# Turning and splitting the residual block by block behind the output projection of a hybrid decoder layer

## The chip, the cores and the metric

One Trainium2 chip, one core of it. The metric is the device time of one execution in microseconds (us). The kernel is one program with one instruction stream per engine: TensorE (PE; PEld is its weight load), VectorE (DVE), ScalarE (ACT), GpSimd (POOL), and SyncE (SP), which here only issues DMA transfers. Engines wait for each other by semaphores; an engine executes its own stream strictly in order, so whatever stands behind a waiting instruction waits too.

## What is computed

One layer of a decoder for 512 prompt tokens and 8 sample tokens together (T = 520 tokens, model width 1024 = 8 blocks of 128 channels). A combined input projection feeds three branches (spatial gating MLP, gated DeltaNet, cross-attention); their gated sum goes through `w_o` and is added to the residual. Then comes a mixture of experts, 4 groups of 8, of which each token takes the top group and two experts in it. The end of the layer, which is what the change is about, is in the reference:

```
x = x + (g_a * o_a + g_b * o_b + g_c * o_c) @ p['w_o']
x = x + hier_moe(rmsnorm(x, p['norm_ffn']), p)
...
grp_logits = (t @ p['w_router_group'] + p['b_router_group']).astype(F32)
g_idx = jnp.argmax(grp_logits, axis=-1)
exp_logits = (t @ p['w_router_expert'] + p['b_router_expert']).astype(F32)
top_v, top_i = lax.top_k(in_grp, TOP_K)
act = jax.nn.silu(gate) * up * combine[:, gi, :, None]
```

All inputs and outputs are fp32. Besides the two residual streams the layer returns memory keys and values, the DeltaNet states (`gdn_s` for the samples), and the last rows of the convolution.

## The kernel before, in words

**Layout.** Activations lie channel-major: the 128 partitions are channels of a block, tokens run along the free axis. SBUF is cut by hand into named regions (`RA`, `M`, `ZG`, `HT`, `CQ`, `MKV`, `RAW`, `X`) that many tensors share one after another; `place` puts a tensor into one.

**Order of work.** A list, `SCHEDULE`, made by `make_schedule` (line 125), gives one order of events. Every engine walks through this list and executes its share of each event, so an engine's order is the order of the list, and the engines meet through semaphores. There is no planner that decides at run time.

**Dense projections.** Weights come in 52 blocks of 1 MiB (`load_block`, line 598) into a ring of three `raw` buffers. ScalarE rounds a block to its high part `w_h` (line 1510), VectorE subtracts to get the low part `w_l` (line 2069), and every product is three: high with high, high with low, low with high (line 900). The last four blocks are `w_o`. Their tiles are numbered `WO_TILE + k`, k = 0 to 7, one for each block of 128 output channels. From k = 2 on a tile comes in two parts of 24 products, so that other work can be put between them. ScalarE's `w_h` and VectorE's `w_l` of the next weight block stand in their streams at part 0 of each even k. When a tile is done VectorE adds the residual: `x1[k]` (line 2143).

**Between the output tiles** stand the updates of the sample states: `sd_diag` (ScalarE, eight copies with a scale, line 1782), `sd_outer` (two products on TensorE, line 1359, then VectorE's addition, line 2462, which also releases the PSUM tensor), `sd_decay` (VectorE, line 2456), and the store of each head by SP (line 627). `f_prep` of block k scales `x1` by `norm_ffn` and rounds it on ScalarE (`hr_h`, line 1792), squares it (line 1793), and has VectorE make the low part `hr_l` (line 2468); GpSimd sums the squares (line 1978). `r_mm` (line 1370) adds the block's share of the 36 router logits, again in three products for each half of the tokens, with the logits on partitions. `f_table` lets GpSimd fill the constants of the expert stage.

**Behind the last tile.** `f_norm` sums the squares per token (line 1380); the logits are copied out and transposed to token rows (lines 1796, 1386); VectorE picks group and experts in a chain of small dependent operations (lines 2481 to 2517) that ends in `hit`; `rank` (line 1430) counts with products of 0 and 1 at which place of its expert's list each token stands; VectorE then has the number of rounds (line 2531), each token's rank, and with `one_hot` the selection matrix `sel` (line 2540). Beside that, `h_in` and `h_sub` turn `x1`, scaled by `norm_ffn`, into five token tiles of 104 rows, which are split into three bf16 parts `h2p` (lines 1406 to 1422 on TensorE, 1808 on ScalarE, 2522 on VectorE).

**Expert stage.** Experts go in 16 pairs. For a pair TensorE gathers the chosen tokens (`gather`, line 1066: 120 products of `h2p` with `sel`; for the first pair `first_gather`, line 1086), ScalarE copies them to `xt` (line 1830), then come gate, up and down products (line 1095), 32 each. A pair needs `e_gate` and `e_up` (4 MiB each) and two `e_down` (2 MiB each), one buffer of each kind. SP reloads a buffer when its last user has finished (`load_pair`, line 633); the loads of the second pair are cut in halves (`load_second`, line 652) and the first of them waits for half of the first pair's gate products (`half_mm`). The first pair itself is loaded by `load_pair(0)`: `e_up` when all output tiles are done, `e_gate` after the logits, `e_down` after `f_norm` and the last `sd_outer`. Results go out by indirect DMA to `y_rows`; the last pair's rows and the residual are added in the final stage, which also normalizes and stores `y`.

## Time and profile before

| | |
|---|---|
| time, median of 3 runs | 1384.88 us (1384.71 to 1386.62) |
| span of the profiled execution | 1385.7 us |
| TensorE busy / weight loads | 1295.6 us (93%) / 1011.1 us (73%) |
| VectorE, ScalarE, GpSimd busy | 485.1, 451.6, 141.1 us |
| chain that ended last, by engine | PE 66%, DMA 20%, DVE 6%, ACT 5%, issue 2% |
| mean granted TensorE clock | 0.983 of full speed |
| HBM read, written | 295.80 MB, 25.10 MB |

The span runs from the first to the last instruction of one profiled execution; the page gives no other time for that execution. TensorE runs at one of two clocks, 1.2 or 2.4 GHz; the granted clock is given as a share of the full one. "Idle before" names what ended the idle time of an engine in front of an instruction; "issue" means that the profile shows nothing it waited for. A busy TensorE is not TensorE at its peak, since products are pipelined and their ends modelled. In the chain, the pieces from about 776 to 841 us are the output projection, those to 872 us the router and the first gather, those to about 1348 us the experts.

### The profile page before, as it was taken

The numbers are of one execution on the slowest core, as the hardware profiler recorded it, in microseconds if no ns is written. First come the engines' busy times: TensorE is split into PE (matmuls) and PEld (weight loads), VectorE is DVE, ScalarE is ACT, GpSimd is POOL, SyncE is SP. The second block draws the span as 40 slices with busy tenths as digits, with TensorE's granted clock in tenths as the row PEclk, the third lists the DMA queues.
The fourth block names the chain that finished last, engine by engine and source line by source line (L and its number), as shares of the span: only waits on it lengthen the run. The fifth ranks groups of instructions, "written<-read, shape, count | busy, mean of one in ns | idle before, by whom it ended". The sixth has DMA issues, their size and how long they took to land.

```text
span 1385.7 us, 24097 instructions
## 1 busy us (share of the span) xinstructions
PE 1295.6 (93%) x10407; PEld 1011.1 (73%) x10407; DVE 485.1 (35%) x882; ACT 451.6 (33%) x775; POOL 141.1 (10%) x208
## 2 busy tenths in 40 slices
PE   3999999899999998989999899999999999999997
PEld 3999988688999998779999888544454444454435
DVE  6332243433346556742344876210010100010003
ACT  5532223443234466344447664101111111011012
POOL 2320000000122211100111112010000000000010
PEclk9999999999999999989999999999999999999999
DMA  5235327533162133432113347899999999999983
GB/s 213 74 108 163 116 94 316 212 140 120 64 222 92 61 100 100 132 100 84 54 39 112 151 154 321 329 401 429 429 431 431 431 431 428 429 431 431 429 284 83
DMA packets 67152, 317.69 MB, mean 229 GB/s; under 512 B 29987, under 2 KB 38563, under 8 KB 44277
## 3 DMA queue, kind: packets, MB, share of 16 engines
q1 hardware_dynamic: 64765, 312.54, 57.8%
q0 software_dynamic: 2304, 3.94, 0.7%
q8 instruction: 65, 1.06, 0.3%
q14 instruction: 18, 0.15, 0.0%
HBM read 295.80 MB, written 25.10 MB: 232 GB/s over the span
## 4 chain that ended last, share of the span: by engine, by line
PE 66%; DMA 20%; DVE 6%; ACT 5%; issue 2%; SPq 0%; POOL 0%; DVEq 0%; ACTq 0%
PE pp L900 34%; DMA e_up<-in_w_up 17%; PE pp L1095 14%; PE pp L1066 2%; PE pp L950 2%; DMA e_down<-in_w_down 1%; DVE w_l L2069 1%; PE pp L1269 1%; PE pp L1289 1%; DMA raw<-in_w_blk 1%; PE pp L1297 1%; ACT w_h L1510 1%; PE pp L1202 1%; PE pp L1454 1%; PE pp L1464 1%
## 5 line engine op out<-in xcount | busy, mean ns | idle before, releaser
L900 PE MATMUL pp<-ht_h,w_h 128*128 128x260 f32 x1280 | 270.6, 293 | 9.1 <-DVE ht_l L2188 9.1
L900 PE MATMUL pp<-ht_h,w_l 128*128 128x260 f32 x1280 | 260.4, 285 | 0.0
L900 PE MATMUL pp<-ht_l,w_h 128*128 128x260 f32 x1280 | 260.4, 285 | 0.0
L900 PEld LDWEIGHTS pp<-ht_h,w_h 128*128 128x128 f32 x1280 | 200.6, 192 | 14.6 <-issue 14.0
L900 PEld LDWEIGHTS pp<-ht_l,w_h 128*128 128x128 f32 x1280 | 200.5, 192 | 0.0
L900 PEld LDWEIGHTS pp<-ht_h,w_l 128*128 128x128 f32 x1280 | 200.1, 191 | 0.0
L2069 DVE TENSOR_TENSOR w_l<-raw,w_h 128x2048 fp32r<-128x2048 f32 x52 | 120.8, 2324 | 103.6 <-ACT w_h L1510 103.5
L1095 PE MATMUL pp<-e_up,xt 128*64 128x512 f32 x512 | 116.6, 609 | 18.1 <-DMA e_up<-in_w_up 18.1
L1095 PE MATMUL pp<-e_down,act_t 128*64 128x512 f32 x512 | 115.1, 602 | 3.3 <-DMA e_down<-in_w_down 3.3
L1510 ACT ACTIVATE w_h<-raw 128x2048 fp32r<-128x2048 f32 x52 | 99.5, 1914 | 56.7 <-PE pp L900 53.1
L1095 PE MATMUL pp<-e_gate,xt 128*64 128x512 f32 x512 | 112.6, 592 | 1.2 <-ACT xt L1830 1.2
L1095 PEld LDWEIGHTS pp<-e_up,xt 128*64 128x64 f32 x512 | 36.3, 140 | 96.1 <-issue 67.7
L1066 PE MATMUL pp<-sel,h2p 104*128 104x128 bf16 x1800 | 105.4, 219 | 0.0
L1066 PEld LDWEIGHTS pp<-sel,h2p 104*128 104x128 bf16 x1800 | 101.9, 98 | 0.2
L1095 PEld LDWEIGHTS pp<-e_gate,xt 128*64 128x64 f32 x512 | 36.8, 137 | 73.8 <-issue 73.5
L1095 PEld LDWEIGHTS pp<-e_down,act_t 128*64 128x64 f32 x512 | 36.3, 138 | 70.2 <-issue 68.7
L2594 DVE SCALAR_TENSOR_TENSOR act_r<-pp,slot_r,sg 128x512 f32<-128x512 f32 x16 | 12.0, 751 | 213.2 <-PE pp L1095 213.2
L2606 DVE TENSOR_SCALAR y_sb<-pp,slot_w 128x512 f32<-128x512 f32 x16 | 12.0, 751 | 202.7 <-PE pp L1095 202.7
L2135 DVE SCALAR_TENSOR_TENSOR cacc<-xpad,params,cacc 128x512 f32<-128x512 f32 x72 | 62.1, 863 | 56.2 <-ACT cacc L1566 54.5
L1842 ACT ACTIVATE act_t<-pp 128x512 f32<-128x512 f32 x16 | 9.6, 597 | 199.7 <-PE pp L1137 199.7
L2013 POOL TENSOR_TENSOR fill<-fill 128x1 f32<-128x1 f32 x47 | 16.3, 353 | 435.8 <-DVE y_sb L2606 273.3
L1563 ACT ACTIVATE xpad<-pp 128x520 f32<-128x520 f32 x24 | 14.5, 605 | 77.5 <-PE pp L900 77.4
(451 smaller groups left out, 1685.8 us busy)
## 6 DMA issues: line engine op xcount, KB each, us to landing
e_up<-in_w_up SPq DMA_DIRECT2D x16, 4096.0 KB, 22.6
e_gate<-in_w_gate SPq DMA_DIRECT2D x15, 4096.0 KB, 20.8
e_down<-in_w_down SPq DMA_DIRECT2D x30, 2048.0 KB, 15.6
raw<-in_w_blk SPq DMA_DIRECT2D x52, 1024.0 KB, 5.1
kv_ring<-in_cache_k SPq DMA_DIRECT2D x8, 1024.0 KB, 5.6
kv_ring<-in_cache_v SPq DMA_DIRECT2D x8, 1024.0 KB, 4.8
s_ring<-in_state_gdn SPq DMA_DIRECT2D x16, 512.0 KB, 5.3
y_rows<-zero_y SPq DMA_DIRECT2D x10, 416.0 KB
```

The lines of the kernel that those rows point to most:

```text
L900: last = mm(dst, w_[:, k, cs], x_[:, k, ts], start=(k == 0 and q == 0), stop=(k == KD - 1 and q == 2))
L950: last = mm(out[:, u, :], lhs(u), rhs(u), start=True, stop=True)
L1066: last = mm(pp[0][:, k // 4, (k % 4) * 128:(k % 4 + 1) * 128], src[:, t, k * 128:(k + 1) * 128], sel[:, t, :, :], start=(i == 0), stop=(i ...
L1095: last = mm(out[rows], lhs[:, rows], w, start=start, stop=stop, skip_group_check=True)
L1202: last = mm(ob[:, c, :], av_tok[:, c, g * 128:(g + 1) * 128], ws_t[:, g, :], start=False, stop=(c == NCH - 1))
L1269: last = mm(dst, qc[:, 2 * h + dc, c * CH:(c + 1) * CH], mk[:, 2 * h + dc, :], start=(dc == 0), stop=(dc == 1))
L1289: last = mm(side[:, dc, :], mv[:, mt, cc:cc + 128], prob_t[:, mt, :], start=(mt == 0), stop=(mt == 1))
L1510: fn(w_h[b % 2][:], raw[b % 3][:], ACT.Copy).then_inc(hi_ready, 1)
L1563: fn(whole(xpad[t % 2][:, 3:3 + T]), ps, ACT.Copy).then_inc(conv_copy, 1)
L2013: return tt(fill[:, 4 + i:5 + i], fill[:, 3:4], fill[:, 3:4], ALU.mult)
L2069: tt(w_l[b % 3][:], raw[b % 3][:], w_h[b % 2][:].bitcast(F32), ALU.subtract).then_inc(lo_ready, 1)
L2135: ins = stt(c_[:, 0:SEQ], x_[:, tap:tap + SEQ], param("w_conv", 4 * SLOT[t] + tap), c_[:, 0:SEQ], ALU.mult, ALU.add)
```

## The change

- **Turned per block.** `x1` is no longer scaled and turned in five token tiles behind the projection. In ten parts (`PARTS`) it is transposed as it is, four 104x128 pieces at a time, into one PSUM bank (`turn_x`); eight of the parts stand between the output tiles, two behind the last. ScalarE rounds the bank to bf16 (first of `h2p`), VectorE subtracts that from the bank (`x_remainder`, `x_rest`), ScalarE rounds the remainder (`x_middle`), and GpSimd subtracts again (`x_lowest`). The next part's transposes wait for the remainder, since there is one bank. `h_in`, `h_sub`, `first_gather`, `gain_d`, `zero_b` and `minus_b` go.
- **Gain elsewhere.** `norm_ffn` is multiplied into the router weights (GpSimd, `w_r_gain`) and into `xt`, which VectorE now writes instead of ScalarE.
- **Logits** are five fp32 products per block with the tokens as stationary side, straight to token rows; `hr_h`, `hr_l`, the split router weights and the transposition of the logits go.
- **`sd_diag`** of odd heads moves to GpSimd, one operation; five of the `sd_outer` steps (heads 3 to 7) move one half tile later.
- **Homes.** `e_gate` lies in `RA`, `e_down[0]` in `ZG`, `h2p` in `HT`, the small tensors of the expert stage in `CQ`. The first pair is loaded in six pieces: `e_down[0]` at `sd_outer` 5, three quarters of `e_up` behind the last state store, and the rest, with `e_gate`, when all output tiles are done. The final loads of `yt` wait for `oh_mm` too.

```diff
+PARTS = [0, 1, 2, 3, "b0", 4, 5, 6, 7, "b1"]
+NPART = len(PARTS)
...
-    out += [("sd_diag", 0), ("w_r_split",), ("f_prep", 0), ("f_prep", 1), ("sd_decay", 0), ("sd_diag", 1)]
-    outers = {(2, 1): 0, (3, 0): 1, (3, 1): 2, (4, 0): 3, (4, 1): 4, (5, 0): 5, (5, 1): 6, (6, 0): 7}
+    out += [("sd_diag", 0), ("w_r_gain",), ("f_prep", 0), ("f_prep", 1), ("sd_decay", 0), ("sd_diag", 1)]
+    outers = {(2, 1): 0, (3, 0): 1, (3, 1): 2, (4, 1): 3, (5, 0): 4, (5, 1): 5, (6, 0): 6, (6, 1): 7}
+    turns = {(2, 0): (0,), (2, 1): (1,), (3, 0): (2,), (4, 0): (3,), (4, 1): ("b0",), (5, 0): (4,), (6, 0): (5,), (7, 0): (6,)}
     for k in range(2, KD):
         for p in range(2):
             out += [("tile", WO_TILE + k, p, 2)] + ([("f_table",)] if (k, p) == (KD - 1, 0) else [])
-            if p:
-                out += [("f_prep", k)] + ([("r_mm", 0)] if k == 2 else []) + [("r_mm", k - 1)]
+            out += [("f_prep", k)] if p else []
+            for part in turns.get((k, p), ()):
+                out += ([("r_mm", part)] if part != "b0" else []) + [("turn_x", PARTS.index(part))]
             if (k, p) in outers:
                 h = outers[k, p]
                 out += [("sd_outer", h)] + ([("sd_decay", h + 1)] if h + 1 < NH else [])
                 out += [("sd_diag", h + 2)] if h + 2 < NH else []
-    out += [("h_in", 0), ("r_mm", KD - 1), ("f_norm",), ("router",), ("h_sub", 0, 0), ("h_in", 1), ("h_sub", 1, 0),
-            ("h_in", 2), ("h_sub", 0, 1), ("rank",), ("h_sub", 0, 2), ("h_in", 3), ("h_in", 4), ("h_sub", 0, 3), ("h_sub", 0, 4),
-            ("moe",), ("final",)]
+    out += [("r_mm", KD - 1), ("turn_x", PARTS.index(KD - 1)), ("f_norm",), ("turn_x", PARTS.index("b1")),
+            ("router",), ("rank",), ("moe",), ("final",)]
...
-        h2p = [place(f"h2p{i}", [TT, NT, D], "RA", 8 * T + i * NT * D // 2, BF16) for i in range(3)]
-        lg_t = place("lg_t", [NG + NE, T], "RA", 8 * T + 3 * NT * D // 2)
+        h2p = [place(f"h2p{i}", [TT, NT, D], "HT", i * NT * D // 2, BF16) for i in range(3)]
+        x_rest = [place("x_rest0", [TT, 4, 128], "HT", 3 * NT * D // 2), place("x_rest1", [TT, 4, 128], "MKV", 288)]
...
+        e_gate = place("e_gate", [128, 2, KD, DE], "RA", 8 * T)
         e_up = place("e_up", [128, 2, KD, DE], "RAW")
-        e_down = [place("e_down0", [128, DE // 128, D], "CQ"), place("e_down1", [128, DE // 128, D], "RAW", 8192)]
+        e_down = [place("e_down0", [128, DE // 128, D], "ZG"), place("e_down1", [128, DE // 128, D], "RAW", 8192)]
...
+            def load_first():
+
+                kh = KD // 2
+                sp.wait_ge(tile_mm, 2 * (NBLK - 1))
+                sp.dma_start(e_up[:, 1], pair("w_up", 1, 1)[:, 0]).then_inc(eu_loaded, 16)
+                sp.dma_start(e_up[:, 0, kh:KD], pair("w_up", 0, 1)[:, 0, kh:KD]).then_inc(eu_loaded, 16)
+                sp.wait_ge(tile_mm, 2 * NBLK)
+                sp.dma_start(e_gate[:], pair("w_gate", 0, 2)).then_inc(eg_loaded, 16)
+                sp.dma_start(e_up[:, 0, 0:kh], pair("w_up", 0, 1)[:, 0, 0:kh]).then_inc(eu_loaded, 16)
+                mmed(sp, ("sd_outer", NH - 1))
+                sp.dma_start(e_down[1][:], pair("w_down", 1, 1)[:, 0]).then_inc(ed_loaded[1], 16)
...
+                    if h == 5:
+                        sp.wait_ge(fin_m, NH)
+                        sp.dma_start(e_down[0][:], pair("w_down", 0, 1)[:, 0]).then_inc(ed_loaded[0], 16)
...
+            sp.wait_ge(oh_mm, rounds)
...
-            def first_gather(n):
-
-                pe.wait_ge(ht_lo, 2)
-                for i in range(2):
-                    mm(pp[0][:, i, :].rearrange("p (u n) -> p u n", u=8), ident_b[0:TT, :],
-                       zero_b[:, 0:64].rearrange("p (o n) -> p o n", o=1).to_broadcast([TT, 8, 64]), start=True, stop=True)
-                pe.wait_ge(sel_ready, n + 1)
-                pe.wait_ge(ht_part, 1)
-                for t in range(NT):
-                    if t >= 3:
-                        pe.wait_ge(ht_lo, t)
-                    for k in range(KD):
-                        for i, src in enumerate(h2p):
-                            last = mm(pp[0][:, k // 4, (k % 4) * 128:(k % 4 + 1) * 128],
-                                      src[:, t, k * 128:(k + 1) * 128], sel[:, t, :, :],
-                                      start=False, stop=True, skip_group_check=True)
-                last.then_inc(gather_mm, 1)
...
-                    pe.wait_ge(h_lo, 16 + k + 1)
-                    for q, (w_, x_) in enumerate(((w_r_h, hr_h), (w_r_l, hr_h), (w_r_h, hr_l))):
-                        for hf in range(2):
-                            last = mm(side_r[0:NG + NE, hf, 0:HALF], w_[:, k, :], x_[:, k, hf * HALF:(hf + 1) * HALF],
-                                      start=(k == 0 and q == 0), stop=(k == KD - 1 and q == 2))
+                    pe.wait_ge(x1_ready, k + 1)
+                    for t in range(NT):
+                        last = mm(side_r[0:TT, 0, t * (NG + NE):(t + 1) * (NG + NE)], x1[:, k, t * TT:(t + 1) * TT],
+                                  w_r[:, k, :], start=(k == 0 and t == 0), stop=True, skip_group_check=True)
...
+                elif e == "turn_x":
+                    n = ev[1]
+                    part = PARTS[n]
+                    if n:
+                        pe.wait_ge(xp_rest, n)
+                    for u in range(4):
+                        if part in ("b0", "b1"):
+                            src = x1[:, u + 4 * (part == "b1"), 4 * TT:NT * TT]
+                        else:
+                            src = x1[:, part, u * TT:(u + 1) * TT]
+                        last = nc.tensor.transpose(part_bank[:, u, :], src, const("ident"))
+                    last.then_inc(xp_turned, 1)
...
+                    pe.wait_ge(rounds_set, 1)
+                    rounds = pe.value_load(n_rounds[0:1, 0:1], min_val=1, max_val=9)
+                    pe.wait_ge(xp_low, NPART)
                     with pe.Fori(0, rounds) as r:
-                        first_gather(r * NPAIR)
+                        gather(r * NPAIR, range(KD))
...
+            def x_middle(n):
+                act.wait_ge(xp_rest, n + 1)
+                fn(part_of(1, n), x_rest[n % 2][:], ACT.Copy).then_inc(xp_mid, 1)
...
-                    fn(hr_h[:, k, :], x1[:, k, :], ACT.Copy, scale=param("norm_ffn", k)).then_inc(h_hi, 1)
                     fn(x_res[:, k, :], x1[:, k, :], ACT.Square).then_inc(sq_ready, 1)
+                elif e == "turn_x":
+                    n = ev[1]
+                    if n:
+                        x_middle(n - 1)
+                    act.wait_ge(xp_turned, n + 1)
+                    fn(part_of(0, n), part_bank, ACT.Copy).then_inc(xp_hi, 1)
...
+            def x_lowest(n):
+                pool.wait_ge(xp_mid, n + 1)
+                tt(part_of(2, n), x_rest[n % 2][:], part_of(1, n), ALU.subtract).then_inc(xp_low, 1)
...
+                elif e == "sd_diag" and ev[1] % 2:
+                    h = ev[1]
+                    if h == 1:
+                        pool.wait_ge(sd_lo, 2)
+                    else:
+                        mmed(pool, ("sd_outer", h - 2))
+                    tt(u_diag[1][:], u_st[:, h:h + 1, :].bitcast(F32).to_broadcast([72, NS, 128]),
+                       const("pick3", 72)[:, 0:NS].rearrange("p (b o) -> p b o", o=1).to_broadcast([72, NS, 128]),
+                       ALU.mult).then_inc(sd_diag[1], 1)
+                elif e == "turn_x":
+                    n = ev[1]
+                    if n:
+                        x_lowest(n - 1)
...
+            def x_remainder(n):
+                dve.wait_ge(xp_hi, n + 1)
+                if n >= 2:
+                    dve.wait_ge(xp_low, n - 1)
+                tt(x_rest[n % 2][:], part_bank, part_of(0, n), ALU.subtract).then_inc(xp_rest, 1)
...
+                elif e == "turn_x" and ev[1] < NPART - 1:
+                    x_remainder(ev[1])
                 elif e == "router":
-                    dve.wait_ge(ht_mm, 1)
-                    copy(h2p[0][:, 0, :].rearrange("p (a n) -> p a n", a=2), pp[H_UNIT[0]][0:TT]).then_inc(ht_hi, 1)
-                    dve.wait_ge(logits_mm, 1)
+                    dve.wait_ge(router_mm, 1)
...
+                    def tokens(n):
+
+                        dve.wait_ge(gather_mm, n + 1)
+                        tt(xt[:].rearrange("p (a k) n -> p a k n", a=2), pp[0][:].rearrange("p a (k n) -> p a k n", n=128),
+                           param("norm_ffn").rearrange("p (a k o) -> p a k o", a=2, o=1).to_broadcast([128, 2, KD // 2, 128]),
+                           ALU.mult).then_inc(xt_ready, 1)
```

## Rows read from the trace of the kernel before

**Rows 1.** Windows; busy us (operations) of five engines; granted clock, DMA share, GB/s.
```profile
870.00:875.00 5.00, 3.80 (x37) 2.12 (x36) 0.50 (x4) 1.02 (x1) 1.40 (x2) 1.00 0.45 184
875.00:880.00 5.00, 5.00 (x29) 1.73 (x27) 0.01 (x1) 0.00 (x0) 0.18 (x1) 1.00 0.53 177
...
900.00:1300.00 400.00, 381.87 (x2977) 186.12 (x2975) 42.86 (x146) 47.61 (x60) 29.18 (x56) 0.99 1.01 427
```

**Rows 2.** The chain of waits in the expert stage: start us, us, what.
```profile
1062.62 22.79 DMA e_up<-in_w_up
```

**Rows 3.** Timeline of the queue SP issues: start us, us.
```profile
876.24 0.38 SPq L655 DMA_DIRECT2D e_gate<-in_w_gate  x1
```

**Rows 4.** The chain of waits from the router to the first pair.
```profile
847.03 0.35 DVE lg L2481
...
852.88 0.33 DVE hit L2517
...
855.83 1.23 DVE h2p L2522
...
859.97 1.95 ACT h2p L1808 x2
...
863.02 8.34 PE pp L1086 x120
...
872.55 7.09 PE pp L1095 x32
```

**Rows 5.** Timeline, VectorE, last output block: x1 of block 7.
```profile
841.08 0.70 DVE L2143 TENSOR_TENSOR x<-pp,x_res 128x520 f32<-128x520 f32 x1 [0.16 <-PE pp L900]
```

**Rows 6.** Timeline, VectorE: the count and the first one-hot.
```profile
856.98 0.18 DVE L2528 TENSOR_REDUCE cnt<-pp 128x1 f32<-128x32 f32 x1
...
858.34 0.83 DVE L2540 TENSOR_TENSOR sel<-consts,rank 104x640 bf16<-104x640 f32 x1
```

**Rows 7.** Timeline, TensorE: fp32 weight loads of 104 and 128 columns.
```profile
764.11 0.42 PEld L955 LDWEIGHTS pp<-consts,qkv 128*128 128x128 f32 x4 [1.14 <-issue]
...
844.36 1.94 PEld L1380 LDWEIGHTS pp<-consts,x_res 128*104 128x104 f32 x20
```

**Rows 8.** Timeline, TensorE: behind a long gap in the delta stage.
```profile
611.30 1.94 PE L995 MATMUL pp<-t_lo,m_t 128*128 128x64 f32 x8 [3.61 <-issue]
```

**Rows 9.** Windows as in Rows 1: granted clock in three stretches.
```profile
615.00:616.00 1.00, 1.00 (x6) 1.00 (x6) 0.41 (x1) 0.00 (x0) 0.00 (x0) 0.50 0.04 16
...
740.00:780.00 40.00, 36.76 (x306) 35.41 (x305) 25.14 (x44) 23.30 (x45) 3.11 (x4) 1.00 0.38 139
...
805.00:810.00 5.00, 5.00 (x30) 4.84 (x29) 2.82 (x4) 2.26 (x8) 0.00 (x0) 0.66 0.70 250
```

**Rows 10.** Timeline, TensorE: the two gaps in the output projection.
```profile
803.56 0.72 PE L1359 MATMUL pp<-u_diag,k_st 72*128 72x512 f32 x2 [1.53 <-DVE small L2464]
...
818.63 1.12 PE L1359 MATMUL pp<-u_diag,k_st 72*128 72x512 f32 x2 [1.82 <-DVE small L2464]
```

**Rows 11.** The chain of waits in the output projection.
```profile
824.26 2.89 PE pp L900 x24
...
827.15 0.71 PE pp L1370 x6
...
827.85 0.46 PE pp L1359 x2
```

**Rows 12.** Timeline, VectorE, around the last weight block.
```profile
808.78 0.70 DVE L2143 TENSOR_TENSOR x<-pp,x_res 128x520 f32<-128x520 f32 x1 [1.62 <-issue]
...
815.03 2.29 DVE L2069 TENSOR_TENSOR w_l<-raw,w_h 128x2048 fp32r<-128x2048 f32 x1 [1.60 <-ACT w_h L1510]
```

**Rows 13.** Timeline: GpSimd beside VectorE in block 6.
```profile
836.67 1.35 POOL L1978 TENSOR_TENSOR x_res<-x_res 128x520 f32<-128x520 f32 x1 [6.00 <-ACT x_res L1793]
...
836.77 2.33 DVE L2471 TENSOR_TENSOR gain_d<-consts,params 128x1024 f32<-128x1024 f32 x1
```

**Rows 14.** Timeline, ScalarE: xt in the expert loop.
```profile
1279.58 1.03 ACT L1830 ACTIVATE xt<-pp 128x1024 f32<-128x1024 f32 x1 [1.08 <-PE pp L1066]
```

195 lines of the change are left out of this document (52 added, 143 removed).

## The prediction

> **What bounds the kernel now.** The windows come first. From 900 to 1300 us the DMA share is 1.01 at 427 GB/s [rows 1]: the expert stage is bound by the weight stream. The chain of waits says the same: from 971 us on nearly every pass waits 20 to 24 us for an `e_up` load [rows 2]. A pair of experts brings 3 x 4 MiB = 12.58 MB, at 427 GB/s 29.5 us. So once the stream runs for good, the end is fixed: what counts is when it starts for good. Before that is a hole. The first pair's weights have landed by about 872.9 (share 0.45 in 870 to 875) and the share is 0.53 in 875 to 880, so the DMA engines stand idle for 0.55 x 5 + 0.47 x 5 = 5.1 us [rows 1], because the queue's next load needs the first half of the first gate products and is issued at 876.24 [rows 3]. From there the end shifts one for one with that moment. The tail behind the last load (about 46 us) is not touched: the new wait on `oh_mm` for `yt` is a wait for work that ends before the last stores.
>
> What sets 876.24 is, going back, the first gate products (872.55), `xt`, the first gather of 8.5 us, then five rounds of turning the residual token-major and splitting it, and the router's serial chain on VectorE from 847.03 to 853.20 [rows 4]. All that hangs from the end of the last output projection at 841.08, when `x1` of the last block is added [rows 5]. I call that end E.
>
> **Behind E: what goes.** Before, against E = 841.08: the router's first VectorE operation at +5.95, `hit` done at +12.1, the count read at +15.9 [rows 6] because VectorE was in the low-part subtractions of `h2p` (855.83 + 1.23 [rows 4]), the gather's products from +21.9 and gate products at +31.47.
> After, in steps of rows: `x1` at +0.70 [rows 5]. Logits of block 7 are 5 products; an fp32 product with a 128x104 stationary tile is taken at 1.94/20 = 0.097 us, so 0.48; the turn of the block is 4 transposes, 0.42; the sums of squares are 10 products, 0.97 [rows 7]. With 0.1 for passing signals, +2.7; `Ln` and `Exp` 0.5; ScalarE also has to square the block and store one middle and one high part ahead of it. Each such part is half of a 1024-wide one (1.95/2 = 0.98 [rows 4]), 0.5 to 0.6. The router starts on VectorE at +3.4, where the remainder of part 8 has ended too. Gained: 2.6, namely the second transposition of the logits, the wide copy before it and `hr_h`.
> The VectorE chain to `hit` is unchanged, 6.2 us [rows 4]: +9.6. Rank products, 0.9: +10.5. Beside them VectorE does the last remainder (half of 1.23: 0.6), so nothing stands between it and the count: +10.6 instead of +15.9. From the count to the end of `sel` is 859.17 - 856.98 = 2.2 [rows 6]: +12.8. Now TensorE waits for that, for the number of rounds (0.8 behind the count, and a register load that I put at 1.2) and for `xp_low` of the last part: exponentials, middle part, low part on GpSimd about +12.1. I take +13.0 for the gather, against +21.9: the 5 x (fill and 8 products with `gain_d`) and the subtractions are gone.
> The gather itself gains nothing. Its 120 products took 8.4 us in the chain, 8.5 with the first of them, with a low clock in part; TensorE now stands still from +4 to +9.6 and again to +13, longer than before. After a gap of 3.6 us the trace shows 8 products in 1.94 us at low clock [rows 8], and at 615 to 616 the granted clock is still at 0.5, the 1.2 GHz level [rows 9]: some 6 us of it from 611 on, which cost 3 us; after the 1.5 us gap of 803.56 it was low for some 3.3 us, costing 1.7 [rows 9, 10]. Taking one such loss off the gather's 8.5 leaves 6.8 for it at full clock, so 8.5 to 9.8 after; I take 9.2: +22.2. `xt` is now one VectorE product with the gain, 1024 wide from PSUM: 1.23 as the same width in [rows 4] instead of 1.03 on ScalarE. Gate products at +23.6, against +31.47: **7.9 us earlier**, with both ends of the gather 7.3 to 8.6; with 1 us of other error either way 6.2 to 9.6.
>
> **The weights of the first pair.** They were no wait before and must not be one now. `e_down[0]` goes out in block 5 and 3 MiB of `e_up` behind the last state store (about E - 5), then gate, rest of up and `e_down[1]` at E. What is left at E - 5 is 10.5 MB, 24.5 us at 427 GB/s: all landed at about E + 21, the gate weights at E + 14. The next load goes out 3.7 us behind the first gate product (876.24 - 872.55), E + 27. In the old places the first pair would have landed at E + 31.8 and eaten 4 to 5 of the 7.9 us. So the early loads are what lets the gain through; their own price is nothing where TensorE has no load to wait for there (the raw blocks are all in by block 4).
>
> **Ahead of E: the output projection.** Here the change adds work. Before, from the end of the first two output tiles, 0.6 before 791.2, to 841.1, 50.5 us: 12 parts of 2.89, 7 logit steps of 0.71, 8 state products of 0.46 [rows 11] = 43.4; a gap of 0.6 at the start, which stays, and two of 1.5 and 1.8 [rows 10]; the rest, 3.2, is the clock, which stands at 0.66 of full speed in 805 to 810 [rows 9], behind the first of these gaps. After: 34.7 + 7 x 0.48 + 3.7 + 8 turns of 0.42 = 45.1, 1.7 more. The gaps of 1.5 and 1.8 go: they were state products waiting for VectorE to release their bank, behind the splitting of `hr`, which is gone, and the fourth state product moves from the first to the second half of block 4.
> A new wait comes. Turn "b0", behind the second half of block 4, shares its bank with the turn before; the bank is free when VectorE has subtracted remainder 3, which stands behind `w_l` of the last weight block, which stands behind ScalarE's square, `u_diag` and `w_h`. In the trace the second half of block 3 ends at 808.5 (the `x` row at 808.78 follows it), and `w_l` ends at 815.03 + 2.29 = 817.3, 8.8 later [rows 12]. With remainder 0.65 that is 9.5. TensorE arrives after 0.46 + 2 x 2.89 + 0.48 + 0.42 = 7.1. The wait is 2.4, or 2.0 as ScalarE is rid of the 0.7 of `hr_h`, and more where GpSimd runs beside: `gain_d`, 1024 wide from SBUF and SBUF, took 2.33 with GpSimd at work for 1.35 beside it [rows 13], 1.1 above the 1.23 of the same width in [rows 4], and GpSimd gets 8 low parts and 4 `u_diag` (1024 wide, 2.1 to 2.7 each) in this stage. One or two such hits: 2 to 4 us, I take 3.0. Such a gap brings a low clock, 1.7. Queued behind that turn is the fourth state product, then block 5; all wait. Sum: 45.1 + 0.6 + 3.0 + 1.7 + 0.3 for small waits = 50.7 against 50.5: **E stays, +0.2**. Ends: no such wait, 45.1 + 0.6 = 45.7, E 4.8 us earlier; a wait of 4 us and two small ones with one more clock loss, E 3 us later.
> One place for the Trainium skill. In [rows 9] the clock was full in 740 to 780 us, with 16 such turns in the stream of products. The page "TensorE: Matmul & The Clock Gate" (Part 4: PE-mode transpose) says that transposes do not count as activity for the clock. By the rule the eight new turns would each invite a low clock; by the row they do not. The row decides, the rule keeps a small chance (third rival).
>
> **The expert loop.** `xt` moves from ScalarE to VectorE, 0.2 longer, behind `rows`, which wait for a store that has long landed; `xt` was ready 1.1 us into the down products (1279.58 + 1.03, [rows 14]), and these 32 take 7.1 as the gate products do [rows 4], so some 5.5 us are spare. Nothing. The stream does not notice.
>
> **Sum.** The profiled execution's span is 1385.7 us, 0.8 above the median of 1384.88. -7.9 + 0.2 = -7.7: span 1378.0, median **1377.2 us**.
>
> **Rivals.** (1) The output projection loses its old gaps and gets no new one: E 4.8 us earlier, 1384.9 - 7.9 - 4.8 = 1372.2. For it: three of the four engines are relieved there; against: the order in which `w_l` and remainder 3 stand. (2) The ring TensorE, ScalarE, VectorE, TensorE binds in more turns, with GpSimd holding up VectorE: E 3 to 5 us later, 1380 to 1382. For it: [rows 13]; against: elsewhere every turn has at least 2.9 us since the last remainder. (3) Slower: each of the eight turns is followed by a low clock. One costs 1.7, as the loss behind 803.56 did; 8 x 1.7 = 13.6 against the 3.2 + 3.3 of clock and gaps before, with 1.7 more work: +8.8, less 7.9, 1385.8. It decides from five or so turns on, with a wait of 3 us at one of them: 1388.8. Against: 740 to 780 us. (4) The stream is not shifted, because something else in it ends last (a store, the last load): 1384.9. Against: a share of 1.01 over 400 us.
>
> **How the numbers follow.** Forecast (1375.5 to 1379.5) 0.5, rival 1 0.2, rival 2 0.17, rival 3 0.08, rival 4 0.05. No change is within 0.2%, 2.8 us: 1382.1 to 1387.7. Faster: 0.5 + 0.2 + 0.15 = 0.85; same 0.02 + 0.05 + 0.03 = 0.10; slower 0.05. The range reaches over rival 1 and into rival 2: 1371.5 to 1382.
>
> **What would show it.** In the changed profile: the chain from the last `x1` to the first gate product at 23 to 25 us instead of 31.5; the queue's load of the second gate weights 7 to 9 us ahead; a DMA hole of 5 to 8 us there; a TensorE gap of 2 to 4 us in front of the turn of "b0", with 1.2 GHz behind it; the distance from that load to the end unchanged within 1 us. The forecast is wrong if E moves by over 3 us, if the gather starts later than E + 15, or if that last distance moves.

## The result

Over 20 runs of each kernel the changed one has a median of 1380.7 us, the kernel before 1384.8; the ratio is 0.9972, with a 95% interval of 0.9959 to 0.9985, so 2.1 to 5.7 us faster. The forecast was 1377.2: the measured time lies inside its range (1371.5 to 1382), but outside the 1375.5 to 1379.5 that it called likeliest, and the gain was put 3.5 us too high (7.7 instead of 4.1 by the medians). Two executions that were far slower than all others count in no ratio of this document: one of the kernel before (2178 us) and one of "half the norm early" (7274 us).

| | before | after |
|---|---|---|
| span of the profiled execution, us | 1385.7 | 1379.2 |
| output projection: first product of block 2 to E | 49.8 | 50.3 |
| E to the first gate product | 31.5 | 25.9 |
| E to the issue of the second gate load | 35.2 | 29.6 |
| from that issue to the end | 509.5 | 509.2 |

E is, as in the prediction, the start of the last residual addition. In the trace of after it lies at 840.43 us, [rows 5] has 841.08 before; but block 2 began at 790.13 against 791.24, in code that the change doesn't touch.

### The profile page after: what moved, and what is told of

Read it like the earlier page. It is cut to its first block, busy times and chain, and to the rows that moved or that the text cites. A ratio compares the mean times of both kernels' runs of the same rounds, so it can differ in the third digit from the quotient of the medians.

```text
span 1379.2 us, 24009 instructions
## 1 busy us (share of the span) xinstructions
PE 1281.9 (93%) x10370; PEld 1000.2 (73%) x10370; DVE 499.8 (36%) x894; ACT 419.8 (30%) x726; POOL 162.8 (12%) x220
## 4 chain that ended last, share of the span: by engine, by line
PE 66%; DMA 20%; DVE 7%; ACT 5%; issue 2%; SPq 0%; POOL 0%; DVEq 0%; ACTq 0%
PE pp L913 34%; DMA e_up<-in_w_up 17%; PE pp L1090 14%; PE pp L1079 3%; PE pp L963 2%; DMA e_down<-in_w_down 2%; DVE w_l L2032 1%; PE pp L1264 1%; PE pp L1284 1%; DMA raw<-in_w_blk 1%; PE pp L1292 1%; ACT w_h L1479 1%; PE pp L1197 1%; PE pp L1423 1%; PE pp L1433 1%
## 5 line engine op out<-in xcount | busy, mean ns | idle before, releaser
L1079 PE MATMUL pp<-sel,h2p 104*128 104x128 bf16 x1920 | 114.0, 221 | 2.6 <-DVE sel L2497 2.6
L1079 PEld LDWEIGHTS pp<-sel,h2p 104*128 104x128 bf16 x1920 | 110.4, 99 | 2.9 <-DVE sel L2497 2.7
L2544 DVE TENSOR_TENSOR xt<-pp,params 128x1024 f32<-128x1024 f32 x16 | 19.6, 1224 | 85.5 <-PE pp L1079 85.5
## 6 DMA issues: line engine op xcount, KB each, us to landing
e_up<-in_w_up SPq DMA_DIRECT2D x15, 4096.0 KB, 22.6
```

Source lines behind the costliest of these rows:

```text
L1079: last = mm(pp[0][:, k // 4, (k % 4) * 128:(k % 4 + 1) * 128], src[:, t, k * 128:(k + 1) * 128], sel[:, t, :, :], start=(i == 0), stop=(i ...
L2544: tt(xt[:].rearrange("p (a k) n -> p a k n", a=2), pp[0][:].rearrange("p a (k n) -> p a k n", n=128), param("norm_ffn").rearrange("p (a k ...
```

## The profile after

Windows (busy us of TensorE, its weight loads, VectorE, ScalarE, GpSimd; granted clock, DMA share, GB/s). They answer [rows 1] and [rows 9]:

```profile
805.00:810.00 5.00, 5.00 (x42) 4.91 (x42) 4.88 (x7) 2.00 (x6) 2.16 (x2) 1.00 0.60 215
815.00:820.00 5.00, 4.17 (x35) 4.08 (x35) 3.25 (x7) 2.27 (x4) 4.06 (x4) 1.00 0.01 3
845.00:850.00 5.00, 0.00 (x0) 0.00 (x0) 4.34 (x16) 1.03 (x3) 4.02 (x9) 0.64 1.06 447
850.00:855.00 5.00, 1.59 (x20) 1.51 (x20) 3.49 (x15) 1.08 (x3) 1.55 (x2) 0.50 0.99 423
855.00:860.00 5.00, 3.73 (x36) 3.74 (x37) 4.55 (x16) 0.20 (x1) 1.09 (x3) 0.50 1.04 439
860.00:865.00 5.00, 4.93 (x87) 4.76 (x85) 1.94 (x6) 0.00 (x0) 0.53 (x2) 0.99 0.79 333
865.00:870.00 5.00, 3.67 (x18) 1.39 (x20) 1.30 (x2) 0.00 (x0) 1.05 (x2) 1.00 0.03 3
870.00:875.00 5.00, 5.00 (x29) 1.66 (x27) 0.93 (x7) 1.43 (x2) 0.10 (x1) 1.00 0.77 285
900.00:1300.00 400.00, 383.44 (x3062) 190.26 (x3059) 58.75 (x164) 34.01 (x46) 27.46 (x54) 1.00 1.01 428
```

Three things are to be seen. The stream fills 900 to 1300 us as before. The hole in it is now 0.21 x 5 + 0.97 x 5 + 0.23 x 5 = 7.1 us (5.1 before): the first pair is there at about 864, and the stream waits for the router. And the clock is full in the output projection, but at 1.2 GHz from 846 to 860, while TensorE does nothing or little.

The queue that SP issues; the last line answers [rows 3] and is 6.2 us ahead of it:

```profile
837.67 0.74 SPq L654 DMA_DIRECT2D e_up<-in_w_up  x1
840.42 0.38 SPq L656 DMA_DIRECT2D e_gate<-in_w_gate  x1
...
870.02 0.38 SPq L664 DMA_DIRECT2D e_gate<-in_w_gate  x1
```

The chain of waits behind E, answering [rows 4] and [rows 6] (start us, us, what):

```profile
840.43 0.71 DVE x L2106
841.18 1.10 PE pp L1364 x10
842.29 0.46 PE pp L1388 x4
842.74 1.76 PE pp L1375 x20
845.13 0.36 DVE lg L2444
846.11 0.83 DVE r L2459
851.62 0.34 DVE hit L2480
852.09 1.45 PE pp L1396 x15
853.71 0.20 DVE cnt L2485
853.94 0.54 DVE cnt L2486
855.38 0.84 DVE sel L2497
856.27 8.68 PE pp L1079 x120
864.97 1.24 DVE xt L2544
866.33 7.09 PE pp L1090 x32
```

The turning and splitting that filled E + 14 to E + 22 is gone from the chain. What stands in it is the router, and between its steps nothing but signals. Two durations are not what rows of before promised: the ten norm products (L1375) take 1.76 us, and a small VectorE operation (L2459) 0.83, where its equal later in the same function takes 0.20.

Ahead of E, one gap of TensorE is left, at the turn that the prediction named. The timeline of that stretch, VectorE, GpSimd and TensorE:

```profile
812.89 2.29 DVE L2032 TENSOR_TENSOR w_l<-raw,w_h 128x2048 fp32r<-128x2048 f32 x1 [1.78 <-ACT w_h L1479]
813.38 2.81 POOL L1842 TENSOR_TENSOR h2p<-x_rest,h2p 104x512 bf16<-104x512 f32 x1 [3.35 <-ACT h2p L1564]
815.10 0.68 DVE L2125 TENSOR_TENSOR x_rest<-pp,h2p 104x512 f32<-104x512 f32 x1
...
815.84 0.65 PE L1388 MATMUL pp<-consts,x 128*104 128x128 f32 x4 [1.50 <-DVE x_rest L2125]
```

A GpSimd subtraction does meet VectorE's split of the last weights here. But VectorE started first, and it is GpSimd that takes longer: 2.81 us, where the same operation takes 1.16 to 1.25 behind E.

## The experiments

All are edits of the changed kernel. Beside the time stand three distances from the trace: the stage (start of block 2 to E), E to the first gate product, and E to the second gate load; "stage + load" is the sum of the first and the third, 85.0 us in the kernel before. "By time" is the ratio of each to the kernel before, times 1384.8. A ratio rests on 12 executions, for the changed kernel on 20, for "turns behind" on 5, for "all" on 7.

| kernel | ratio, 95% interval | by time | stage | gate | load | stage + load, against before |
|---|---|---|---|---|---|---|
| changed kernel | 0.9972 (0.9959-0.9985) | -3.9 | 50.3 | 25.9 | 29.6 | -5.1 |
| the same again | 0.9979 (0.9965-0.9994) | -2.9 | 50.3 | 26.7 | 30.4 | -4.3 |
| late loads | 0.9997 (0.9981-1.0013) | -0.4 | 50.2 | 26.6 | 30.3 | -4.5 |
| turns behind | 1.0087 (1.0058-1.0117) | +12.0 | 45.2 | 47.6 | 51.3 | +11.4 |
| busy TensorE | 0.9957 (0.9942-0.9972) | -6.0 | 50.3 | 24.4 | 28.1 | -6.6 |
| fifth turn later | 0.9974 (0.9957-0.9991) | -3.6 | 50.1 | 26.7 | 30.4 | -4.5 |
| half the norm early | 0.9958 (0.9944-0.9972) | -5.8 | 50.3 | 26.2 | 29.9 | -4.9 |
| GpSimd held | 0.9969 (0.9954-0.9984) | -4.3 | 50.3 | 26.4 | 30.1 | -4.6 |
| spread on ScalarE | 0.9971 (0.9956-0.9986) | -4.0 | 50.4 | 26.6 | 30.3 | -4.4 |
| both edits ahead of E | 0.9967 (0.9950-0.9984) | -4.6 | 49.5 | 27.0 | 30.7 | -4.8 |
| router's edits | 0.9944 (0.9927-0.9962) | -7.8 | 50.3 | 22.6 | 26.2 | -8.4 |
| router's edits, late loads | 0.9968 (0.9949-0.9988) | -4.4 | 50.3 | 23.3 | 28.7 | -6.1 |
| all | 0.9937 (0.9915-0.9959) | -8.7 | 49.5 | 22.6 | 26.3 | -9.3 |

Read the last column against "by time": one for one within 1.4 us, save for the two kernels with late loads. So the sum of two stretches of one trace says within that margin what the time will do, which the span of one trace can't: in the changed kernel and its variants the start of block 2 lay anywhere from 788.6 to 793.2 us, and the stretch from the second gate load to the end took 504.7 to 509.2, both in code that is the same in all.

**The same kernel again.**

> The changed kernel once more, so that the next three stand beside it on one chip, and so that its distances have a second trace. The stage from block 2 to E should take 50.3 us again, the first gate product come at E+25.9 within 0.5, and the time lie 2 to 6 us below the kernel before. What is open is the stretch from the second gate load to the end: 509.5 us in the kernel before, 509.2 in the changed kernel's first trace, but 508.0, 506.3 and 506.6 in the first experiments, which change nothing in it. If it differs by over 1 us between two traces of the same code, the stretch isn't rigid from run to run, and single spans can't carry a difference of this size.

The last stretch took 507.5 us, where the first trace of this code has 509.2. So it moves by over 1 us with nothing changed, and "unchanged within 1 us" was no test that one pair of traces could fail. The gather's time moves too: from its first product to `xt` 8.7 us in the first trace, 9.5 in this, as the clock came back 3.8 us behind the gather's first product there and 5.4 here.

**The weights in their new homes, loaded as late as before.**

```
 def load_first():
-    sp.wait_ge(tile_mm, 2 * (NBLK - 1))     # three quarters of e_up
+    sp.wait_ge(tile_mm, 2 * NBLK)           # all of e_up
+    sp.wait_ge(router_mm, 1)                # then e_gate
+    mmed(sp, ("f_norm",)); mmed(sp, ("sd_outer", NH - 1))   # then both e_down
...
-    if h == 5: e_down[0]
```

> The changed kernel with its weights in the new homes, but the first pair loaded as late as in the kernel before: all of the up projection behind the last output projection tile, the gate behind the last router product, both down projections behind the norm's products and the last outer product. Distances count from E, the end of the last residual addition. Theory after the changed kernel's trace: the load then has only its 12.58 MB to move in the router's 25.9 us (29.5 us at 427 GB/s), it lands at about E+32, where it lands at E+24 now, and the second gate load could be issued at E+29.6 anyway, so 2 to 2.5 us of the stream's idle stretch are all that is lost: the second gate load at E+31 to E+33, the time 1 to 3.5 us above the changed kernel's. The rival, which the prediction held: 4 to 5 us are lost. A second rival: nothing is lost, since the router and not the load sets the first gate product. In all three E moves by less than 0.5 us.

The trace shows no loss: the second gate load goes out at E + 30.25, as in the repeat of the changed kernel, and the DMA engines have moved as many bytes by E + 100 (46.5 MB from E - 45 on, against 46.4 and 46.8). The hole is filled instead. By time it lost 2.5 to 3.5 us, though the intervals of the two touch. The forecast's 4 to 5 us are out by the trace, 0 to 3.5 stay open. One trace may not stand for the rest: the profiled execution took 1382.8 us, 2.0 less than the median of its kernel. Each execution also has a mean granted clock on record, and in every kernel here the slower executions tend to have the lower one, by about 1 us for 0.001. With late loads its median is 0.979 and the profiled execution has 0.981, as the changed kernel's two series have in the median. That would fit more time at 1.2 GHz in most of the executions that were not profiled; no trace shows it.

**All turns behind the projection.**

```
-    out += ([("r_mm", part)] if part != "b0" else []) + [("turn_x", PARTS.index(part))]
+    out += [("r_mm", part)] if part != "b0" else []
...
-    out += [("r_mm", KD - 1), ("turn_x", PARTS.index(KD - 1)), ("f_norm",), ("turn_x", PARTS.index("b1")),
-            ("router",), ...
+    out += [("r_mm", KD - 1), ("f_norm",)] + [("turn_x", n) for n in range(NPART)] + [("router",), ...
```

> The changed kernel with the router's products where they are, but all ten turned parts of the residual behind the last output projection instead of in the gaps of the tiles. It measures what the eight turns cost in the stage and what their place saves. Theory: the stage from the start of block 2 to E becomes 50.3 - 8 x 0.38 (the turns) - 1.5 (the gap ahead of the fifth) = about 45.7 us, and the ten turns with their copy to bf16, subtraction and second wait (some 2 us for one, through one bank) then stand ahead of the logits on VectorE: the first gate product moves from E+25.9 to E+42 to E+46, the time is 11 to 17 us above the changed kernel's. Rival: the turns lie beside the router's own chain, which mostly waits for semaphores; then E falls by the 4.6 us and the first gate product comes at E+30 to E+34, and the time is 0 to 4 us above. A second rival: E falls by less than 3 us, because the turns were hidden under the tiles.

The time is 15.9 us above the changed kernel's, as the theory had it (11 to 17); the first gate product is later than it had it (E + 47.6 against E + 42 to E + 46). The stage shrinks by 5.1 us, so the eight turns and the gap of the fifth cost that, 8 x 0.38 for the turns, 1.5 for the gap, 0.6 in small pieces; behind E they make a ring of one bank with a period of 2.51 us, and the first gate product comes 21 to 22 us later than in the changed kernel. Timeline of VectorE in this kernel:

```profile
839.56 0.69 DVE L2125 TENSOR_TENSOR x_rest<-pp,h2p 104x512 f32<-104x512 f32 x1 [4.12 <-ACT h2p L1768]
842.06 0.69 DVE L2125 TENSOR_TENSOR x_rest<-pp,h2p 104x512 f32<-104x512 f32 x1 [1.81 <-ACT h2p L1768]
844.57 0.69 DVE L2125 TENSOR_TENSOR x_rest<-pp,h2p 104x512 f32<-104x512 f32 x1 [1.81 <-ACT h2p L1768]
```

What the change wins is the place of these turns, not their form: by time the new form behind the projection is 12 us slower than the kernel before, and the place is worth 16 us.

**TensorE kept busy.**

```
+            def warm(n):      # bf16 products that nothing reads, into the bank of the gather
+                for _i in range(n):
+                    mm(pp[0][:, 0, :]..., ident_b[:], mask_b[:, 0:1, :].to_broadcast([128, 4, 128]), ...)
...
 elif e == "rank":
+    warm(26)
     ...
     last.then_inc(rank_mm, 1)
+    warm(8)
```

> The changed kernel with products that nothing reads (bf16, 128 columns of weights by 512) on TensorE while it waits for the router: 26 ahead of the ranks, 8 between the ranks and the gather. They leave the router's chain on VectorE as it is. The changed kernel's trace has the clock at 1.2 GHz from E+6 to E+20: the ranks take 1.6 us instead of 0.9 and the gather 8.7 where the kernel before has 8.34 with half of it slow. Theory: the clock fell because TensorE was idle; with it busy the ranks are 0.7 us shorter and the gather takes 6.3 to 7.3 us, the first gate product comes at E+23 to E+24 and the time is 1.5 to 3 us below the changed kernel's (the expert loop follows one to one). Rival: the level is granted by something else than TensorE's own work in this stretch (the clock stays at 1.2 GHz); then the 26 products take 11 us instead of 5.6, the ranks start 4 to 5 us late and the time is 4 to 5 us above. Second rival: the gather is shorter but the time stays, since the first pair's load sets the first gate product.

Timeline of this kernel, TensorE, VectorE and GpSimd:

```profile
848.46 6.88 PE L856 MATMUL pp<-mask_b,ident_b 128*128 128x512 bf16 x26
...
856.54 1.16 POOL L1850 TENSOR_TENSOR h2p<-x_rest,h2p 104x512 bf16<-104x512 f32 x1 [2.88 <-ACT h2p L1572]
856.61 1.12 DVE L2494 TENSOR_SCALAR cnt<-consts,cnt 128x8 f32<-128x8 f32 x1
...
859.52 6.87 PE L1085 MATMUL pp<-sel,h2p 104*128 104x128 bf16 x120 [1.45 <-DVE sel L2505]
```

The gather takes 6.87 us, all at 2.4 GHz, and the ranks 0.9: the low clock came from TensorE having nothing to do. The clock did fall once, at 847.3 behind the sparse norm products, and came back at 850.7 under the 26 products. So the low clock costs 1.8 to 2.5 us in the gather (8.67 and 9.41 us for its 120 products in the two traces of the changed kernel) and 0.7 in the ranks. What the shorter ranks gave was taken back at once: the count now met a GpSimd operation, and an 8-column VectorE operation took 1.12 us, 0.23 where no GpSimd operation is beside it and 0.53 in the changed kernel. It ends at 857.73, the GpSimd operation at 857.70. By time this kernel is 2.1 to 3.1 us below the two readings of the changed one, with intervals that overlap; what the clock costs is read from the traces.

**The fifth turn in a later gap.**

```
-PARTS = [0, 1, 2, 3, "b0", 4, 5, 6, 7, "b1"]
+PARTS = [0, 1, 2, 3, 4, "b0", 5, 6, 7, "b1"]
-    turns = {... (4, 1): ("b0",), (5, 0): (4,), (6, 0): (5,), ...}
+    turns = {... (5, 0): (4,), (5, 1): ("b0",), (6, 0): (5,), ...}
```

> The changed kernel with the turn that waited (the last tokens of the first four blocks) moved from the gap behind the first half of block 4, where VectorE and ScalarE split the last weights, to the gap behind the second half of block 5. Theory: TensorE's 1.5 us idle ahead of that turn go and nothing of their kind comes, because VectorE's subtraction is then done before TensorE arrives: the stage from the start of block 2 to E takes 48.6 to 49.0 us instead of 50.3, and the time is 1 to 1.7 us below the changed kernel's. Rival: the ring of one bank is the bound, so that the wait turns up again at the next turn (block 5 or 6), the stage stays within 0.4 us of 50.3 and so does the time.

The rival was right on the size and wrong on the place: the 1.5 us went, and 1.3 came back, not at a turn but at two state products that wait for VectorE. Timeline of TensorE:

```profile
829.25 0.73 PE L1354 MATMUL pp<-u_diag,k_st 72*128 72x512 f32 x2 [0.45 <-DVE small L2433]
833.69 0.73 PE L1354 MATMUL pp<-u_diag,k_st 72*128 72x512 f32 x2 [0.84 <-DVE small L2433]
```

**The odd heads' spread back on ScalarE.** The condition of `sd_diag` on ScalarE loses its `ev[1] % 2 == 0`, and GpSimd's branch goes.

> The changed kernel with one part undone: the spread of the odd heads' vectors is done by ScalarE again (8 x 0.3 us a head), not by GpSimd (1.89 us). Theory: GpSimd's work beside VectorE is what stretched VectorE's decay multiplications (1.97 and 2.55 us instead of 1.22 in the changed kernel's trace), and VectorE is the engine that the waits of this stage end on; with the spread on ScalarE, VectorE's busy time in the stage falls by 2 to 4 us, but ScalarE, busy all through the stretch where it splits the last weights, copies the turned parts later: the wait ahead of the fifth turn grows from 1.5 to 3 to 4 us and the stage takes 51.5 to 53 us, the time 1 to 2.5 us more. Rival: ScalarE has room (24.7 of 50 us), the wait shrinks or stays, and the stage takes 49.5 to 50.4 us; then the move to GpSimd bought nothing.

The rival: the stage stays (50.35), the gap too (1.50). ScalarE had room (34.7 us busy of 50), and the move to GpSimd bought nothing that can be seen. It cost VectorE something: the decay multiplication took 1.41 us in the mean instead of 1.59.

```profile
L2416 DVE TENSOR_TENSOR s_ring<-s_ring,s_bc 128x1024 f32<-128x1024 f32 x8 | 11.2, 1406 | 0.3
```

The same group of lines (790 to 840 us) in the changed kernel:

```profile
L2425 DVE TENSOR_TENSOR s_ring<-s_ring,s_bc 128x1024 f32<-128x1024 f32 x8 | 12.7, 1592 | 0.3
```

**Both edits ahead of E.**

> The changed kernel with both edits ahead of E: the turn that waited stands behind block 5's second half, and ScalarE again spreads the odd heads' vectors. Each alone left the stage where it was (50.1 and 50.35 us against 50.3): with the turn moved, TensorE's wait came back ahead of the last two outer products (0.45 and 0.84 us, for VectorE), and with the spread on ScalarE the 1.5 us ahead of the turn stayed. Theory: VectorE is late for the outer products because GpSimd's work stretches it (39.2 us busy in 50, 36.5 with the spread on ScalarE); with both edits neither wait is left and the stage takes 48.8 to 49.3 us, the time 1 to 1.5 us below the changed kernel's. Rival: a third wait takes their place (ScalarE's copies of the turned parts, behind its spread), and the stage stays at 49.9 to 50.5 us.

The stage is 49.5 us, 0.8 shorter, between theory and rival; of the waits one of 0.53 is left, at a state product. So each of the two edits only bared the other's limit, and together they give half of the gap back. By time 0.8 us can't be told.

**Half of the norm's products early.**

```
-    out += [("r_mm", KD - 1), ...
+    out += [("f_half",), ("r_mm", KD - 1), ...     # k = 0 in f_half, k = KD - 1 in f_norm
```

> The changed kernel with the first half of the norm's products (those over the sum of the first seven blocks' squares, which is ready early) ahead of the last block's router products, where TensorE waits 0.79 us for the last residual addition. Theory: a product of float32 operands takes two passes, which is why the norm's ten take 1.76 us; five of them (0.85 us) go under that wait, the logits start at E+3.9 to E+4.1 instead of E+4.70, and the time is 0.6 to 0.9 us below. Rival: the products are only as long as what stands behind them allows (the second turn), or the sum of squares isn't ready that early; then the logits stay at E+4.5 to E+4.9.

The logits start at E + 3.79, 0.91 earlier, and the gather at E + 14.96, 0.88 earlier. But the first gate product comes at E + 26.17, between the two traces of the changed kernel: the gather took 9.8 us, because the clock came back 6.2 us behind its first product. So what the edit gives ahead of the gather can be lost again to the low clock, and its worth shows only where TensorE is kept busy. By time it reads 1.9 to 2.9 us below the changed kernel, more than the trace has, with intervals that overlap.

**GpSimd held until the hits are written.**

```
 elif e == "router":                 # GpSimd
+    pool.wait_ge(hit_ready, 1)
+    x_lowest(NPART - 2); x_lowest(NPART - 1)      # both were elsewhere
```

> The changed kernel with GpSimd held back until the hits are written: its last two subtractions of the residual's third part and the split of the norm's factor come behind the hits instead of beside the logits. Theory: the small VectorE operation that took 0.82 us instead of 0.20 did so because GpSimd's subtraction ran beside it, and hits come at E+10.5 to E+10.7 instead of E+11.19; but two of GpSimd's subtractions then lie beside the count and the selection, which may lose 0.3 to 0.6, so that the gather stands at E+15.2 to E+15.8 (now +15.84) and the time is 0 to 0.7 us below. Rival: the 0.82 us has another cause, and the hits stay at E+11.1 to E+11.3.

The hits start at E + 10.51 instead of 11.19; the operation in question takes 0.20:

```profile
848.70 0.20 DVE L2461 TENSOR_TENSOR r<-lg,r 104x20 f32<-104x20 f32 x1
```

In the changed kernel the same operation ended when GpSimd's did (846.93 and 846.88), as the timeline shows:

```profile
845.63 1.25 POOL L1842 TENSOR_TENSOR h2p<-x_rest,h2p 104x512 bf16<-104x512 f32 x1 [2.08 <-ACT h2p L1564]
845.90 0.17 DVE L2458 TENSOR_REDUCE r<-lg 104x5 f32<-104x20 f32 x1
846.11 0.82 DVE L2459 TENSOR_TENSOR r<-lg,r 104x20 f32<-104x20 f32 x1
```

So it is not slowed in proportion: by these ends it waits for the whole GpSimd operation. The Trainium skill says this of the two engines (page "SBUF — State Buffer", section "SBUF: two separate sides"): their shared ports go to one instruction as a whole, and the other blocks. These rows agree for VectorE operations with both inputs in SBUF, and for the 8-column operation above; in the split of the last weights, above, it is GpSimd that waits. Beside GpSimd's bf16 copies of 0.88 us and its 5-column subtractions of 0.40 us no such stretch shows in the changed kernel's trace, and why is not shown. Of the 0.7 us that the hits win, 0.4 reach the gather (E + 15.42), since a later VectorE operation now meets GpSimd; by time nothing can be told.

**The router's edits together.** 20 and 8 idle products, the half norm early, GpSimd's second to last part behind the hits, and the last one on VectorE:

```
     x_remainder(NPART - 1)
+    dve.wait_ge(xp_mid, NPART)
+    dve.wait_ge(xp_low, NPART - 1)
+    tt(part_of(2, NPART - 1), x_rest[(NPART - 1) % 2][:], part_of(1, NPART - 1), ALU.subtract).then_inc(xp_low, 1)
     dve.wait_ge(rank_mm, 1)
```

> The changed kernel with what the first seven runs point to behind E, all at once: products that nothing reads ahead of the ranks (20) and of the gather (8), the first half of the norm's products under the wait for the last residual addition, GpSimd's second to last subtraction behind the hits, and the last one on VectorE while it waits for the ranks. Three runs of the changed kernel's own code (or of code that differs ahead of E only) had the first gate product at E+25.9, 26.7 and 26.7, the gather taking 8.7, 9.4 and 9.5 us with the clock at 1.2 GHz for its first 3.7 to 5.1 us. Theory (the sum): logits E+3.8 (-0.9), hits E+9.7 (0.6 more, the operation no longer stretched by GpSimd), selection started at E+12.6 to E+13.0 (ranks 0.7 shorter, count 0.3 to 0.8 shorter), gather from E+13.5 in 6.9 us, first gate product at E+22 to E+22.7; the second gate load is issued at E+25.5 to E+26.5, the time is 3.5 to 5 us below the changed kernel's, 6 to 9 below the kernel before. Rival: the stream, not the router, decides: the first pair lands at E+24 and its down projections are needed later only, but if the second gate load's early issue only lengthens the wait later in the loop, the time stays within 1 us of the changed kernel's. Second rival: the clock falls again between the ranks and the gather, the gather takes 8.5 us and the time is 2 to 3 us below.

As summed, but for the selection, which starts at E + 13.3, some 0.3 late: VectorE's own subtraction waits for ScalarE's middle part and ends 0.7 us behind the ranks, which takes back most of what the shorter count gives. Gather at E + 14.15 in 6.87, first gate product at E + 22.55, second gate load at E + 26.24. By time 1377.7 us, -7.8 against the kernel before. The end follows the start of the stream, and the stream's bytes say the same: 48.0 MB between E - 45 and E + 100, 1.2 to 1.5 MB more than the changed kernel, 2.8 to 3.6 us at 428 GB/s. Windows of this kernel; the hole is 3.6 us now (0.68 x 5, and 0.04 x 5 behind it):

```profile
860.00:865.00 5.00, 3.47 (x62) 3.31 (x61) 3.38 (x8) 0.00 (x0) 0.36 (x2) 1.00 1.05 447
865.00:870.00 5.00, 5.00 (x24) 1.66 (x24) 0.00 (x0) 0.00 (x0) 1.22 (x2) 1.00 0.32 95
870.00:875.00 5.00, 5.00 (x29) 1.70 (x27) 1.87 (x9) 1.97 (x2) 0.19 (x1) 1.00 0.96 387
```

**The same with late loads.**

> The previous kernel with the first pair's loads as late as in the kernel before. In the changed kernel this cost nothing by the trace (second gate load at E+30.25, where two traces of the changed kernel have E+29.6 and E+30.35) while its time said some 3 us with an interval that nearly reaches zero. Theory: the first pair's bytes need 30 us behind E by themselves (12.58 MB at 427 GB/s, issued in steps up to E+4.6); a router of 26 us just covers them, one of 22 doesn't: VectorE's and TensorE's times behind E stay those of the previous kernel, the second gate load is issued at E+25.5 to E+26.5 too, but its bytes come behind the first pair's, so that the DMA queues have no idle stretch and the end is that of a load at E+30.5: 4 to 5 us above the previous kernel, within 1 us of the first late-load run. Rival: the time is within 1 us of the previous kernel's, since later waits of the expert loop swallow the difference; then early loads buy nothing in any of these kernels.

2.6 us slower in the median, 3.3 by the ratio, with intervals that overlap; the expectation had 4 to 5. The trace has the second gate load 2.4 us later, and 47.1 MB moved instead of 48.0. There is no hole any more:

```profile
860.00:865.00 5.00, 2.88 (x52) 2.70 (x49) 3.01 (x7) 0.00 (x0) 0.77 (x2) 1.00 1.00 426
865.00:870.00 5.00, 4.84 (x16) 1.55 (x18) 0.00 (x0) 0.00 (x0) 0.63 (x1) 0.66 0.99 421
870.00:875.00 5.00, 5.00 (x29) 1.59 (x27) 0.62 (x6) 0.96 (x1) 0.12 (x1) 1.00 0.99 413
```

And TensorE does wait, against the expectation that its times would stay, for the gate weights, which are second in the queue, and then works at 1.2 GHz for a while:

```profile
865.16 8.78 PE L1095 MATMUL pp<-e_gate,xt 128*64 128x512 f32 x32 [2.28 <-DMA e_gate<-in_w_gate]
```

So by the traces early loads are worth something only when the router is shorter than the load of what its first user needs: the gate weights land at E + 23.3 when loaded late, earlier than the long router lets the first gate product start (E + 26.6) and later than the short one does (E + 22.6). The times don't settle it, for they give late loads the same loss with either router, 2.5 to 3.5 us with the long one and 2.6 to 3.3 with the short one.

**Everything.**

> The last run: the router's edits (first gate product at E+22.55, second gate load at E+26.24, where two traces of the changed kernel have E+29.6 and E+30.35) together with the two edits ahead of E, which brought the stage from 50.3 to 49.5 us. They touch different stretches, so the gains should add: the stage 49.3 to 49.7 us, the first gate product at E+22.4 to E+22.8, the time 0.5 to 1 us below that of the router's edits alone, near 1377 us, 8 to 9 below the kernel before; by timing alone that last step can't be told from nothing. Rival: the spread on ScalarE delays the last turned parts, the logits or the first gate product come later than E+3.9 and E+22.9, and the stage's gain is given back behind E.

1375.7 us in the median (7 runs), ratio 0.9937, 8.7 us below the kernel before; the stage is 49.5 us and the gate product comes at E + 22.56, so the gains add in the trace. It beats both kernels; against the router's edits alone the gain of about 1 us is inside the interval.

## Why the prediction came out as it did

**The frame held.** The end follows the issue of the second gate load, and nothing else in the change shows: with +0.5 in the stage and 4.8 to 5.6 less behind E the traces give -4.3 to -5.1, the times -2.9 and -3.9, each with 2 us of uncertainty. Rival 4 (the stream not shifted) is out by the experiments that shift it on purpose, from -9.3 to +11.4 us. Rival 1 is out: a gap was there, at the named turn. Rival 2 (E 3 to 5 us later) named 1380 to 1382, and 1380.7 lies in it; the time alone would fit it, but the trace doesn't: one turn waited, not several, and the stage is 0.5 us longer. Rival 3 is out: the clock is at full speed in the whole stage, with eight turns in it and a gap of 1.5 us. The Trainium skill's rule on transposes ("TensorE: Matmul & The Clock Gate", Part 4), out of which the prediction made this rival, brought no low clock here: eight groups of four transposes, 0.38 us a group, left it full. The prediction took more from [rows 9] than they say, though: the 16 in 740 to 780 us are single transposes, as many as four turns have.

**The step that failed is the price of an fp32 product.** The prediction took it as 0.097 us, 1.94 / 20 of [rows 7]. But the 20 are records, not products: `f_norm` has two blocks by five token tiles, ten products, in the kernel before as well, and its 1.94 us was the time of those ten. An fp32 product with 104 columns of weights leaves two records and takes 0.17 to 0.19 us. So the norm takes 1.76 us, not 0.97, and each logit step 0.85, not 0.48. Behind E the norm is 0.8 us longer and the logits of block 7, which come out of an idle stretch, 0.6 (1.11 until the turn starts); that is all of the 1.3 us by which the logits are late (E + 4.70 against + 3.4). In the stage it is 7 x 0.37 = 2.6 us; turns, at 0.38, were priced right.

**Three smaller terms behind E**, all with the same sign:
- VectorE's chain to the hits took 6.8 us, not 6.2: the 0.6 us of waiting for GpSimd. The forecast saw such contention ahead of E, in [rows 13], and gave it to no small operation behind E.
- The ranks took 1.6 us at the low clock, not 0.9: the idle TensorE was named, and priced for the gather alone.
- The count lost 0.3 to GpSimd's last part.

With 1.3 they make the gather 2.8 late (E + 15.84 against + 13.0), beyond the E + 15 that was to be the mark of a wrong forecast. The gather (8.7 and 9.5 us against 9.2) and `xt` were right. The register load of the number of rounds, feared at 1.2 us, was hidden.

**The stage came out right by errors that cancel.** Forecast 50.7, from the end of the first two output tiles; by that reading 50.3 + 0.6 = 50.9. The wait at turn "b0" was 1.5 us and not 3.0. VectorE's split of the last weights ended 7.9 us behind the second half of block 3, not 8.8, as ScalarE was free earlier, and it took the same 2.29 us as before, as the GpSimd subtraction beside it was the one that waited. No low clock followed, forecast 1.7, though behind a gap of the same length before, at 803.56, it did in [rows 9, 10]; what makes the difference is not shown. These 3.2 us less are offset by 2.6 for the logits and about 0.8 in small pieces that I did not resolve further (a state product right behind a turn takes 0.55 us of the stream, not 0.46).

**The signs.** Of those that the prediction named, the DMA hole (7.1 us) and the unchanged stretch behind the second gate load (509.2 against 509.5) came, though the latter was luck, as the second trace of the same code has 507.5. The chain from the last `x1` to the first gate product (25.9 and 26.7, not 23 to 25), the earlier second gate load (4.8 to 5.6 us against E, not 7 to 9), the gap (1.5, not 2 to 4) and the 1.2 GHz behind it did not.

**The loads.** The forecast said that late loads would eat 4 to 5 of 7.9 us. In the traces they ate nothing with the router of 26 us and 2.4 us with the one of 22.5; by time 2.5 to 3.5 and 2.6 to 3.3.

What stays open: why the late loads by themselves read 2.5 to 3.5 us slower by time and not at all in the trace; the lower mean clock of those executions is a lead, not an answer.

## What to carry to other kernels

Count the instructions in the source before dividing a row by its count of records: fp32 products leave two each. When a chain of small operations replaces dense work ahead of a dense stage, TensorE can start that stage at 1.2 GHz, as it did here, and products that nothing reads, in its idle time, can be worth more than the next edit of the chain. And where single runs scatter by more than the effect, compare the sums of the stretches that the change touches, between two events that both traces have, not the spans.
